# Modulation rows stored with their bias and spread by DMA, and all token numbers from one one-hot product, in a two-block transformer kernel

## The reference, cut to what matters

```python
for i in range(2):
    mod_l = silu(c) @ w_ada[i] + b_ada[i]            # one row of 6144 for the latents
    mod_c = silu(c_ctx) @ w_ada[i] + b_ada[i]        # and one for the context
    sh1, sc1, g1, sh2, sc2, g2 = split(mod, 6)       # of each
    hl, hc = xl * (1 + sc1_l) + sh1_l, xc * (1 + sc1_c) + sh1_c
    al, ac = attention(hl, hc)                       # layer 0 window GQA, layer 1 differential
    xl = layer_norm(ALPHA * xl + g1_l * al, ln_attn_g, ln_attn_b)
    hl2 = xl * (1 + sc2_l) + sh2_l
    y = moe_ffn(hl2 (and hc2 in layer 0))            # 16 experts, each token goes to 2
    xl = layer_norm(ALPHA * xl + g2_l * y, ln_ffn_g, ln_ffn_b)
```

## Time and profile before

| | |
|---|---|
| median of 3 runs | 2777.28 us (2773.38 to 2780.35) |
| profiled execution | 2782.37 us, span 2780.5 us |
| mean granted TensorE clock | 0.923 of full speed |
| PE, PEld | 2463.1 us (89%), 1941.7 us (70%) |
| DVE, ACT, POOL | 1642.8 us (59%), 1347.3 us (48%), 114.6 us (4%) |
| DMA | 575.69 MB, mean 207 GB/s |

### The profile page before, as it was taken

One profiled execution on the slowest core, in us unless ns is written; L12 is line 12 of the kernel. 1 busy time (PEld: TensorE's weight loads), 2 busy tenths in 40 slices (PEclk: granted clock), 3 DMA queues, 4 the chain that ended last, 5 costly groups with the idle time before them and its releaser, 6 DMA issues. The chain is left out here.

```text
span 2780.5 us, 29917 instructions
## 1 busy us (share of the span) xinstructions
PE 2463.1 (89%) x11670; PEld 1941.7 (70%) x11670; DVE 1642.8 (59%) x2430; ACT 1347.3 (48%) x2030; POOL 114.6 (4%) x118
## 2 busy tenths in 40 slices
PE   8999889999999989998999868999859977999962
PEld 6887667888887767787766546888647655778731
DVE  5556246555556355555435476889684567888802
ACT  5555345555555444554234315777622524777700
POOL 0001000000001000000000000000021000000000
PEclk9999889999999899999899877999969987999976
DMA  7664545665665345665225425999832024999842
GB/s 257 237 218 152 216 170 167 222 226 197 227 212 197 116 159 182 219 222 187 68 99 183 138 89 200 377 390 383 336 134 91 17 91 175 363 378 381 343 182 85
DMA packets 171433, 575.69 MB, mean 207 GB/s; under 512 B 14476, under 2 KB 23116, under 8 KB 139004
## 3 DMA queue, kind: packets, MB, share of 16 engines
q1 hardware_dynamic: 152832, 505.13, 51.2%
q10 hardware_dynamic: 11816, 44.29, 3.9%
q0 software_dynamic: 6624, 24.12, 2.5%
HBM read 526.22 MB, written 47.28 MB: 206 GB/s over the span
## 5 line engine op out<-in xcount | busy, mean ns | idle before, releaser
L371 PE MATMUL PS<-HI,FR 128*128 128x512 f32 (+2 forms) x2144 | 837.4, 391 | 49.9 <-DVE FR L415 24.8
L373 PE MATMUL PS<-HI,FR 128*128 128x512 f32 (+2 forms) x2144 | 827.3, 386 | 0.0
L372 PE MATMUL PS<-LO,FR 128*128 128x512 f32 (+2 forms) x2144 | 827.0, 386 | 0.0
L315 DVE TENSOR_TENSOR LO<-RAW,HI 128x1024 fp32r<-128x1024 f32 x558 | 660.2, 1220 | 275.1 <-ACT HI L301 273.7
L301 ACT ACTIVATE HI<-RAW 128x1024 fp32r<-128x1024 f32 x558 | 569.0, 1053 | 435.7 <-PE PS L373 313.6
L371 PEld LDWEIGHTS PS<-HI,FR 128*128 128x128 f32 x2144 | 411.6, 192 | 144.3 <-DVE FR L415 28.8
L301 ACT ACTIVATE HI<-RAW,SM 128x512 fp32r<-128x512 f32 (+2 forms) x576 | 361.2, 681 | 305.6 <-PE PS L373 201.2
L317 DVE SCALAR_TENSOR_TENSOR LO<-RAW,SM,HI 128x512 fp32r<-128x512 f32 (+2 forms) x576 | 379.5, 710 | 211.5 <-ACT HI L301 211.5
L373 PEld LDWEIGHTS PS<-HI,FR 128*128 128x128 f32 x2144 | 410.8, 192 | 80.8
L372 PEld LDWEIGHTS PS<-LO,FR 128*128 128x128 f32 x2144 | 411.7, 192 | 76.5
L415 DVE TENSOR_TENSOR FR<-PS,FR 128x512 fp32r<-128x512 f32 x224 | 144.9, 676 | 132.0 <-ACT FR L411 131.7
(11 more groups left out here) (283 smaller groups left out, 2049.7 us busy)
## 6 DMA issues: line engine op xcount, KB each, us to landing
RAW<-in_w_ffn_in SPq DMA_DIRECT2D x88, 1024.0 KB, 5.2
RAW<-in_w_gate SPq DMA_DIRECT2D x68, 1024.0 KB, 7.8
RAW<-in_w_up SPq DMA_DIRECT2D x68, 1024.0 KB, 7.3
RAW<-in_w_down SPq DMA_DIRECT2D x68, 1024.0 KB, 8.6
RAW<-in_w_ada SPq DMA_DIRECT2D x48, 1024.0 KB, 4.9
RAW<-in_w_ffn_out SPq DMA_DIRECT2D x44, 1024.0 KB, 4.9
RAW<-in_w_in SPq DMA_DIRECT2D x44, 1024.0 KB, 5.1
YD<-CN ACTq DMA_DIRECT2D x24, 1024.0 KB, 4.8
```

The costliest lines, as they stand in the source:

```text
L315: e.tensor_tensor(LO[:, i % NSPLIT, c], raw_of(j)[:, c], hi, ALU.subtract).then_inc(*lo_done.up())
L371: e.matmul(o, h, hi[:, j, :], start=first and k + j == 0, stop=False)
L372: e.matmul(o, h, lo[:, j, :], start=False, stop=False)
L373: x = e.matmul(o, ll, hi[:, j, :], start=False, stop=end)
```

## The change

The bias is added once, when a group is stored: ACT loads it to the buffer of the group beforehand (two DMAs), DVE adds the PSUM bank to it (in place of ACT L717), and two DMAs store it in place of four. Each row that is needed is then loaded by one DMA that writes it to all 128 partitions (`act_row`, 512 KB; 20 of them, some 10 MB): four hidden rows and the two gates of o0 at the start of the first block's last feed-forward, four fold rows at the start of o0, two gates and four fold rows at the head of m0, the gate of o1 at the start of qb, two fold rows in o1, one gate in m1. `pe_spread` and all that it served is gone. The fold is three operations on 1024 columns in place of six on 512, and that of m0 stands among the experts (before expert 4 and before expert 6) rather than behind them. The latents' hidden rows in qa are computed straight from the last norm (gain times 1+sc first), not from the normed tiles.

The token numbers of all experts and overflows come from one product: 8 one-hots of the place in its tile (128x128) against 8 of tile and expert times the token number (128x64 in m0; 4 of 128x32 in m1). The loop and the further bodies have no such step any more.

```diff
-                e.activation(stage[v], PS[5][:, :], ACT.Copy).then_inc(*act.up(f"mod {l}{g}"))
-                q.wait_ge(*act.last())
-                for j in range(4):
-                    c = 2048 * g + 512 * j
-                    e.dma_start(MOD[l, :, c:c + 512], stage[v][32 * j:32 * j + 2, :]).then_inc(*mod_out[v].up(by=16))
+                for r in range(2):
+                    e.dma_start(stage[v][r:P:32, :], A["b_ada_2"][l, 2048 * g:2048 * g + 2048].rearrange(
+                        "(j c) -> j c", j=4)).then_inc(*bias_in[v].up(by=16))
+                bias_in[v].also(f"bias {l}{g}")
...
+                q.wait_ge(*dve.at(f"mod {l}{g}"))
+                for r in range(2):
+                    e.dma_start(MOD[l, r, 2048 * g:2048 * g + 2048].rearrange("(j c) -> j c", j=4),
+                                stage[v][r:P:32, :]).then_inc(*mod_out[v].up(by=16))
...
+                e.tensor_tensor(stage[v], PS[5][:, :], stage[v], ALU.add).then_inc(*dve.up(f"mod {l}{g}"))
...
-        def act_rows(e, q, l, sec):
-
-            for g in (sec, sec + 1):
-                q.wait_ge(*mod_out[side[l, g]].at(f"mod {l}{g}"))
-            e.dma_start(RR[2:3, :], A["b_ada_2"][l:l + 1, 3072 * sec:3072 * sec + 3072]).then_inc(*r_in.up(by=16))
-            e.dma_start(RR[0:2, :], MOD[l, :, 3072 * sec:3072 * sec + 3072]).then_inc(*r_in.up(f"rows {l}{sec}", by=16))
+        def act_row(e, q, landed, event, l, which, sec, dst):
+
+            q.wait_ge(*mod_out[side[l, sec // 2]].at(f"mod {l}{sec // 2}"))
+            e.dma_start(dst, spread_rows(MOD[l, which:which + 1, 1024 * sec:1024 * sec + 1024])).then_inc(
+                *landed.up(event, by=16))
...
-            act_rows(e, q, 0, 0)
+            for w in range(2):
+                act_row(e, q, hid_in[w], None, 0, w, 1, h_sc[w])
+                act_row(e, q, hid_in[w], f"hid rows {w}", 0, w, 0, h_sh[w])
             e.dma_start(XC[:, :, :], A["ctx_2"][0].rearrange("(t p) d -> p t d", p=P)).then_inc(
                 *ctx_in.up("ctx", by=16))
+            for w in range(2):
+                act_row(e, q, g1_in[w], f"o0 gate {w}", 0, w, 2, o_gate[0][w])
...
+            e.scalar_tensor_tensor(h_sc[0], h_sc[0], 1.0, GB[:, 0, :], ALU.add, ALU.mult).then_inc(*dve.up("hid gain"))
...
+                e.scalar_tensor_tensor(HB[:, t, :], XL[:, t, :], rs[t], h_sc[0], ALU.mult, ALU.mult).then_inc(*dve.up())
+                q.wait_ge(*dve.last())
+                e.tensor_tensor(HB[:, t, :], HB[:, t, :], h_sh[0], ALU.add).then_inc(*dve.up(f"qa hid {t}"))
...
-        def pe_spread(e, q, name, which, col, rows, rot, users):
-
-            b = pe_bank(q, name, rot)
-            q.wait_ge(*r_in.at(f"rows {rows}"))
-            pe_free(q, b)
-            e.matmul(PS[b][:, :], C["bl" if which == 0 else "bc"][0:3, :], RR[:, col:col + 512], start=True,
-                     stop=True).then_inc(*pe.up(name))
-            freed[b] = users
...
+        def dve_fold(e, q, s, which, G, B, T):
+
+            q.wait_ge(*fold_in[which].at(f"{s} fold rows {which}"))
+            q.wait_ge(*gain_in[0].at(f"b {s}"))
+            q.wait_ge(*gain_in[1].at(f"g {s}"))
+            if which:
+                q.wait_ge(*dve.at(f"{s} fold 0"))
+            e.scalar_tensor_tensor(T, G, 1.0, GB[:, 0, :], ALU.add, ALU.mult).then_inc(*dve.up())
+            q.wait_ge(*dve.last())
+            e.tensor_tensor(B, B, T, ALU.add).then_inc(*dve.up())
+            e.scalar_tensor_tensor(G, G, 1.0, GB[:, 1, :], ALU.add, ALU.mult).then_inc(*dve.up(f"{s} fold {which}"))
...
-            pe_gates(e, q, s, range(len(tiles) // 2), f"{l}0", rot)
...
-                if h == 0:
-                    for which in range(len(tiles) // 2):
-                        pe_fold(e, q, s, which, f"{l}1", rot)
...
+            for w in range(len(tiles) // 2):
+                act_fold_rows(e, q, s, l, (4, 3), w, *o_fold[w])
...
+        def pe_places(e, q, l, rot):
+
+            s, n, w = f"m{l}", 2 * X_TILES[l], 16 * X_TILES[l]
+            b = pe_bank(q, f"{s} tokens", rot)
+            q.wait_ge(*dve.at(f"{s} hot"))
             pe_free(q, b)
-            for t in range(NT):
-                x = e.matmul(PS[b][:, 0:1], x_hot[t], C["tid"][:, t:t + 1], start=t == 0, stop=t == NT - 1)
-            return x
-
-        def dve_places(e, q, l, k, j):
-            posm = x_z[5][:, 0:16 * X_TILES[l]]
-            return [(x_hot[t], posm[:, 16 * t + k:16 * t + k + 1]) for t in range(X_TILES[l])]
+            for i in range(n):
+                x = e.matmul(PS[b][:, 0:w], x_row[i], x_tid[i][:, 0:w], start=i == 0, stop=i == n - 1)
+            x.then_inc(*pe.up(f"{s} tokens"))
+            freed[b] = [(dve, f"{s} index")]
...
+            e.tensor_scalar(col, sl, 1.0 / P, -127.0 / 256.0, ALU.mult, ALU.add).then_inc(*dve.up())
+            q.wait_ge(*dve.last())
+            e.tensor_scalar(col, col, 12582912.0, None, ALU.add).then_inc(*dve.up())
+            q.wait_ge(*dve.last())
+            e.tensor_scalar(col, col, -12582912.0, None, ALU.add).then_inc(*dve.up())
+            q.wait_ge(*dve.last())
+            e.scalar_tensor_tensor(row, col, -float(P), sl, ALU.mult, ALU.add).then_inc(*dve.up())
+            q.wait_ge(*dve.last())
+            row, col = (x.rearrange("p (k t) -> p k t", k=2) for x in (x_gs[:, 0:8], x_gsel[:, 0:8]))
+            for i in range(2 * NT):
+                e.tensor_scalar(x_row[i], C["iota"], row[:, i // NT, i % NT:i % NT + 1], None, ALU.is_equal).then_inc(*dve.up())
+                e.tensor_scalar(x_tid[i][:, 0:16 * NT], C["iota"][:, 0:16 * NT], col[:, i // NT, i % NT:i % NT + 1],
+                                C["tid"][:, i % NT:i % NT + 1], ALU.is_equal, ALU.mult).then_inc(*dve.up())
+            dve.also(f"{s} hot")
+            q.wait_ge(*pe.at(f"{s} tokens"))
+            e.tensor_copy(IDX[:, 0:16 * NT], PS[bank[f"{s} tokens"]][:, 0:16 * NT]).then_inc(*dve.up(f"{s} index"))
...
-                for t in range(X_TILES[l]):
-                    x = e.matmul(PS[7][:, 0:1], x_hot[t], C["tid"][:, t:t + 1], start=t == 0, stop=t == X_TILES[l] - 1)
-                x.then_inc(*more_pe.up(f"{s} tokens"))
             more_yd.also(f"m{l} all")
 
         def dve_further(e, q, l):
-            posm = x_z[5]
-
             def first():
                 q.wait_ge(*pe.at(f"m{l} done"))
 
             def one(k, j, s):
-                for t in range(X_TILES[l]):
-                    e.tensor_scalar(x_hot[t], C["iota"], float(P * j), posm[:, 16 * t + k:16 * t + k + 1], ALU.add,
-                                    ALU.is_equal).then_inc(*more_dve.up())
-                more_dve.also(f"{s} hot")
-                q.wait_ge(*more_pe.at(f"{s} tokens"))
-                e.tensor_copy(IDX[:, 16 * j + k:16 * j + k + 1], PS[7][:, 0:1]).then_inc(*more_dve.up(f"{s} index"))
...
+                act_row(e, q, g2_in[w], f"{s} gate {w}", l, w, 5, HBS[w])
+                if l == 0:
+                    act_fold_rows(e, q, s, 1, (1, 0), w, *x_fold[w])
...
+                if l == 0 and i in (4, 6):
+                    dve_fold(e, q, s, i // 6, *x_fold[i // 6], x_fold_t)
...
-                q.wait_ge(*dve.at(f"{s} index {i}"))
+                q.wait_ge(*dve.at(f"{s} index"))
...
```

204 lines of the change are left out of this document (64 added, 140 removed).

## The result

| | before | changed |
|---|---|---|
| median of 4 runs each | 2778.82 us (2773.38 to 2786.58) | 2757.03 us (2749.35 to 2758.70) |
| ratio of the runs, 95% interval | | 0.9918 [0.9896, 0.9940] |
| profiled execution, its span | 2782.37, 2780.5 | 2758.70, 2756.9 |

The changed kernel is 0.8 per cent faster. The prediction was 2745 in 2730 to 2767: the time lies in the range, 12 us behind the forecast. The profiled spans differ by 23.6 us, where the sum said 32.8. So the sum can't be judged by its total. It has to be judged stage by stage, and there two terms were wrong and one place that I had at nothing cost 2 to 3 us, others made up for them, and a few us come and go from run to run.

The account below looks back on a forecast made before the run. The prediction took DMA to bound the expert loops and the chain PE, ACT, DVE the heads and joints. Its terms summed to -32.8 us, from 2777.3 to 2744.5, rounded to 2745, range 2730 to 2767.

Parts of the forecast that it names:

- Rival 1: Expert loops of m0 and m1: PE sets their pace, so removed places' matmuls count, 23 us; 2722 in all; chance 0.08.
- Start of qa: Head of qa: latents' chain to the projections 5.9 us earlier, less 1.9 for a cold-clock start; -4.0 us.
- o0, -7.1 and -12.2: o0: start without the gates' products, -7.1 us; between halves no three-row matmuls and no cold spell, -12.2 us.
- o1, -9.3: o1: same two edits as o0 at half size, -2.2 us at the start and -7.0 between the halves.
- Heads, +3.5 and +2.3: Heads of m0 and m1: first index copied later, behind the one product for all token numbers; +3.5 and +2.3 us.
- Loop of m0: m0's expert loop: folds stall PE about 2.6 us each, caught up if DMA sets the pace; +1.0 us.
- Behind m0's experts: After m0's experts: without the fold DVE starts when ACT's copy is ready; -3.9 us.
- Further bodies: m1's further bodies: gathers go out earlier, gaining 3.4 us in the second and 1.6 in the first; -5.0 us.
- Start of ffn3: Start of ffn3: ACT issues seven DMAs instead of three, 0.41 us each, ahead of its first copies; +1.9 us.
- colder starts: Joints: idle PE stays at the low clock longer than counted, four starts at 1.9 us, +8; 2753; chance 0.10.
- Crowded: m0's loop: folds not caught up (+5) and spread rows fall into the loop (+8); 2758; chance 0.18.
- Slower: Stages wait for the twenty spread rows, 2.5 us a row, +50; 2795; chance 0.06.

Follow-up runs that it names:

- e3: Changed kernel, but m0's two folds made behind its last expert instead of before experts 4 and 6; 2753.22 us.
- e6: Changed kernel, but POOL sends the further bodies' gathers as soon as their buffer is free; 2743.03 us.
- second set: The changed kernel run again as it is, with a second profiled execution; median of 6 runs 2749.19 us.
- e2: Changed kernel with the old places (comparison, product and index for each expert), so only the rows by DMA; 2748.90 us.
- e4: Changed kernel, but ACT's seven DMAs at the start of the last feed-forward spread behind its first four blocks; 2746.78 us.
- e7: Changed kernel with late rows, folds behind m0's experts, early gathers, and the one-hot product started pair by pair; 2724.23 us.
- e8: As e7, but the first two experts get their token numbers the old way; 2729.78 us.
- e10: Changed kernel with old places by expert, late rows and folds behind m0's experts, without early gathers or pairs; 2735.07 us.
- e11: Changed kernel with the one product, late rows and folds behind m0's experts, without early gathers or pairs; 2742.44 us.
- e1_onehot_only: Kernel before the change with only the token numbers from one product, no rows spread by DMA; 2777.74 us.

## Why the prediction was right, and where it was wrong

**The bound.** Right. The expert loops are DMA's: PE 4 per cent less busy in m0 (I had said two), with the share still at 0.98. Rival 1 (23 us from the loops) would need 15.2 in m0 alone; the one product gained 4.7 there and nothing of its own in m1.

**Start of qa, -4.0.** The chain is shorter by 8.5 us rather than 5.9. From the four L640 to the last L415 the changed kernel takes:

```profile
1312.74 2.73 DVE L640 SCALAR_TENSOR_TENSOR XL<-PS,XL 128x512 f32<-128x512 f32 x4 [1.56 <-PE PS L569]
...
1336.48 0.69 DVE L415 TENSOR_TENSOR FR<-PS,FR 128x512 fp32r<-128x512 f32 x1 [0.16 <-ACT FR L411]
```

The hidden rows of the latents were ready only 0.4 us sooner than I had summed (the changed kernel lags by 6.5 us here, which is taken off). The largest part of the 2.6 is ACT's exponential, for which I had 2.2 us behind the norms:

```profile
1316.72 1.28 ACT L1264 ACT_TABLE_LOAD   x1
...
1325.34 0.20 ACT L1264 ACTIVATE SM<-SM 128x2 f32<-128x2 f32 x1 [7.34 <-DVE SM L1286]
```

The load of its table ran while DVE still made the hidden rows, so only 0.8 us were left behind the norms. The other half of the step, the cold start at 1.9, came as forecast in the changed kernel (its projections cost 2.0, at a clock of 0.50 until 1340) and at 1.5 in e3 and e6, and not in the second set, in e2, e4, e7, e8, e10 and e11. So both figures of the step stand beside each other in one kernel: -6.5 in one execution, -8.7 in another. By the Trainium skill ("TensorE: Matmul & The Clock Gate", Part 4: PE-mode transpose) the clock would stay low in all of them, since transposes are all that PE has there. In `e4_rows_late` it rises while only they run:

```profile
1326.00:1330.00 4.00, 2.57 (x11) 2.17 (x12) 3.97 (x5) 1.19 (x2) 0.00 (x0) 0.50 0.00 0
1330.00:1332.00 2.00, 1.09 (x7) 0.85 (x5) 1.36 (x3) 1.45 (x3) 0.00 (x0) 0.83 0.00 0
1332.00:1334.00 2.00, 1.43 (x6) 1.24 (x7) 2.00 (x3) 0.67 (x1) 0.00 (x0) 1.00 0.00 0
```

PE's timeline of the same kernel, in which nothing but L392, the transposes, runs between 1315.55 and the first product at 1332.57:

```profile
1327.00 1.97 PE L392 MATMUL PS<-CN,HB 128*128 128x128 f32 x8 [7.04 <-DVE HB L1321]
1329.40 1.69 PE L392 MATMUL PS<-CN,HB 128*128 128x128 f32 x8 [0.43 <-DVE HB L1321]
1332.57 0.47 PE L371 MATMUL PS<-HI,FR 128*128 128x512 f32 x1 [1.48 <-DVE FR L415]
```

The measurement decides: here transposes did raise the clock.

**o0, -7.1 and -12.2, and o1, -9.3.** Right, within 0.8 us in o0 in all profiled executions of kernels with the rows. For o1 -9.1 and, in the second execution, -6.9, and -9.2 to -10.6 in the others. Between o1's halves it is 7.1 us in all of them, as forecast; what varies lies in the attention ahead of it, with which the stage of the table begins.

**Heads, +3.5 and +2.3.** Right: +4.7 and +4.1, +2.9 and +2.8. PE took 3.68 us for m0's product where I had 3.75.

**Loop of m0, +1.0.** Right in the mechanism (a stall at the folds, part of it caught up) and in size, +0.8 and -1.1. But the catching up is slow. Of the 3 to 4 us lost at experts 4 to 6 half or less came back by 1990, so my own sign of being wrong, a stall still there at expert 15, holds for the other half. The size came out right because the loop had gained 1.3 and 3.1 us before the first fold, for which I had no term. `e2_rows_only` shows the stall without that room, 9.1 us.

**Behind m0's experts, -3.9.** Right: -3.6 and -3.9, DVE following ACT's copy at once.

**Further bodies, -5.0.** This step failed. It measured +0.5 in one execution and -3.8 in the other, and `e1_onehot_only`, `e2_rows_only` and `e10_old_places`, with and without the product, have -3.4, -2.0 and -2.9, so the product gives nothing there that stands out from the differences between runs. I had let POOL be free at the store of the body before, 4.4 us ahead of the old gather. It sent the gather 3.2 us behind that store, so 1.2 were gained and not 4.4, and the same 1.2 in the first body. There the gather also took 9.1 us to the transposes where it had taken 7.2, behind the body's weights, and in the second 8.9 as against 8.8. In `e6_gather_ahead` the place gave 15.2, and its second gather, sent 11 us behind the weights of the body before rather than with its own, landed 4.5 us after its issue.

**Start of ffn3, +1.9.** This term was mis-sized: +6.4 and +6.1, outside the bounds that ended at +3. I priced an issue of a 512 KB spread row by the 0.41 us of the context's load, and counted neither that issues in a row take longer (1.0 each from the fifth) nor the clock that falls while PE has nothing. `e4_rows_late` took 6.2 of the 6.4 back.

**qa's attention, 0.** Mis-sized too: +3.4 and +2.3, the longer cold spell above. I had a rival for colder starts, but no term.

**What made up for it.** What the head of qa gave beyond its term, 2.5 and 4.7 us, and 4.1 us in m1's loop, where I had 0. The latter stands in kernels with and without each half (e10 has +0.9, the others -2.5 to -5.1), so it is not shown to come from the change. That the sum comes so near in the second execution is in this part luck.

**The rivals.** Crowded (2758) named the time nearly right and its reason half right. The folds are caught up only in part, but the rows of m0 did not fall into its loop, where the share stayed at 0.98 and the rate was 375 GB/s as against 379. Colder starts (2753): half right as well. Not at the starts of o0 and o1, which came near their terms, but at ffn3 (2.3 of its 6.4) and at the end of qa's attention (some 2 us) the clock stayed low for longer than I had counted. Slower (2795) fell: 20 rows land in 7.6 and 6.6 us, but it was to decide from 2.1 us of waiting for each, and DVE waits for no landed row. The one thing that stands behind them is ACT at ffn3, and it waits for their issue.

## What to carry to other kernels

A transfer by DMA in place of an engine's work is free only if its issue is: put the issues where their queue has nothing due behind them, a few at a time, and count the clock that PE loses while it waits. An index that is known early gains little (here 1.2 us) until the gather that uses it also goes out early, ahead of the bulk weights of the same stage. Before work is moved into a loop that DMA paces, look for room on the engine that it goes to: at the two folds 9 us were lost with the places' work beside them, 3 to 4 without it, and 1 at most at a place where DVE was waiting.
